# Two transformer blocks in one kernel: how the position bias gets its diagonals, and five places where TensorE waited

## The reference

```python
bias = rel_bias[t5_bucket(t[:, None] - s[None, :])]   # 16 heads, 256 distances
s = q @ k * HEAD_DIM ** -0.5 + bias
u = causal_depthwise_conv(a * sigmoid(gate), conv_w, conv_b)
u = silu(layer_norm(u, ln_g, ln_b))
c_q, c_kv = rmsnorm(c_q, ...), rmsnorm(c_kv, ...)     # block 2, latent stage
```

## Time and profile before

| | |
|---|---|
| median of 3 runs | 2812.84 us |
| profiled execution | 2812.7 us, span 2810.9 us |
| TensorE (PE) busy | 2788.9 us, 99% |
| VectorE (DVE), ScalarE (ACT), GpSimd (POOL) busy | 1949.3, 1377.6, 165.2 us |
| granted TensorE clock, mean | 0.999 |
| DMA, of 16 engines' span | hardware queue 59.5%, GpSimd's queue 0.2% |
| HBM read, written | 505.9 MB, 2.1 MB |

### The profile page before, as it was taken

One profiled execution on the slowest core, in us unless ns is written; L12 is line 12 of the kernel. 1 busy time (PEld: TensorE's weight loads), 2 busy tenths in 40 slices (PEclk: granted clock), 3 DMA queues, 4 the chain that ended last, 5 costly groups with the idle time before them and its releaser, 6 DMA issues.

```text
span 2810.9 us, 45292 instructions
## 1 busy us (share of the span) xinstructions
PE 2788.9 (99%) x15285; PEld 2388.5 (85%) x15285; DVE 1949.3 (69%) x2984; ACT 1377.6 (49%) x1865; POOL 165.2 (6%) x81
## 2 busy tenths in 40 slices
PE   8999999999999999999999999999999999999998
PEld 7888988888888888888888888888888888888887
DVE  6988787866885787778866777777655555555555
ACT  5336755544554455655544555554454434443444
POOL 6770010000000000000000000000000000000000
PEclk9999999999999999999999999999999999999999
DMA  9865365666665665655555565655566556555654
GB/s 246 211 160 130 95 175 184 186 209 189 187 191 193 185 192 189 185 146 152 160 184 177 174 183 172 180 172 187 190 202 190 189 191 195 188 189 194 190 190 154
DMA packets 506528, 509.64 MB, mean 181 GB/s; under 512 B 89662, under 2 KB 405934, under 8 KB 505902
## 3 DMA queue, kind: packets, MB, share of 16 engines
q1 hardware_dynamic: 505774, 506.01, 59.5%
q0 software_dynamic: 560, 2.12, 0.2%
q10 hardware_dynamic: 80, 0.01, 0.0%
HBM read 505.90 MB, written 2.12 MB: 181 GB/s over the span
## 4 chain that ended last, share of the span: by engine, by line
PE 99%; DVE 0%; ACT 0%; DMA 0%; issue 0%; ACTq 0%; SPq 0%; DVEq 0%
PE banks L1928 34%; PE banks L1931 17%; PE banks L1958 12%; PE banks L1959 12%; PE banks L1960 12%; PE banks L1943 3%; PE banks L1904 2%; PE banks L1945 1%; PE banks L1912 1%; PE banks L2194 1%; PE banks L1913 1%; PE banks L1914 1%; PE banks L2008 0%; PE banks L2325 0%; PE banks L2375 0%; PE banks L2129 0%
## 5 line engine op out<-in xcount | busy, mean ns | idle before, releaser
L602 ACT ACTIVATE w_two<-w_raw 128x1024 fp32r<-128x1024 f32 x944 | 995.1, 1059 | 1146.1 <-PE banks L1960 555.6
L1078 DVE TENSOR_TENSOR w_two<-w_raw,w_two 128x1024 fp32r<-128x1024 f32 (+1 forms) x881 | 1075.3, 1229 | 656.3 <-ACT w_two L602 650.5
L1928 PE MATMUL banks<-hp,w_two 128*128 128x512 f32 x3200 | 1014.1, 398 | 1.0 <-issue 1.0
L1931 PEld LDWEIGHTS banks<-hp,w_two 128*128 128x128 f32 x3200 | 601.4, 188 | 140.2
L1931 PE MATMUL banks<-hp,w_two 128*128 128x256 f32 x3200 | 632.0, 278 | 0.0
L1928 PEld LDWEIGHTS banks<-hp,w_two 128*128 128x128 f32 x3200 | 489.7, 189 | 9.3 <-issue 5.7
L1958 PE MATMUL banks<-w_two,yp 128*128 128x512 f32 x1056 | 412.1, 390 | 0.0
L1960 PE MATMUL banks<-w_two,yp 128*128 128x512 f32 x1056 | 411.2, 389 | 0.0
L1959 PE MATMUL banks<-w_two,yp 128*128 128x512 f32 x1056 | 411.1, 389 | 0.0
L1094 DVE TENSOR_REDUCE arena<-banks 128x256 f32<-128x512 f32 x304 | 195.1, 684 | 55.4 <-PE banks L1931 50.0
L1960 PEld LDWEIGHTS banks<-w_two,yp 128*128 128x128 f32 x1056 | 198.3, 188 | 41.3
(11 more groups left out here) (310 smaller groups left out, 2418.8 us busy)
## 6 DMA issues: line engine op xcount, KB each, us to landing
w_raw<-in_w_in SPq DMA_DIRECT2D x480, 256.0 KB, 3.1
w_raw<-in_w_up SPq DMA_DIRECT2D x352, 256.0 KB, 2.9
w_raw<-in_w_down SPq DMA_DIRECT2D x176, 256.0 KB, 3.0
w_raw<-in_w_ffn_gate SPq DMA_DIRECT2D x176, 256.0 KB, 2.8
w_raw<-in_w_ffn_up SPq DMA_DIRECT2D x176, 256.0 KB, 2.9
w_raw<-in_w_ffn_down SPq DMA_DIRECT2D x176, 256.0 KB, 3.2
w_raw<-in_w_out SPq DMA_DIRECT2D x128, 256.0 KB, 3.6
w_raw<-in_w_mla_proj SPq DMA_DIRECT2D x64, 256.0 KB, 3.0
```

What stands on the lines that cost most here:

```text
L602: nc.scalar.activation(w_hi[:, s, 0:n], w_raw[:, s, 0:n], ACT.Copy).then_inc(hi_ready, 1)
L1078: v.tensor_tensor(w_lo[:, s, 0:n], w_raw[:, s, 0:n], w_hi[:, s, 0:n].bitcast(f32), ALU.subtract)\
L1928: mm(banks[:, b, :], w_hi[:, s, at:at + P], rhs[:, k0 + k, :], start=k0 + k == kt_first, stop=False)
L1931: ins = mm(banks[:, b, 0:T], w_lo[:, s, at:at + P], rhs[:, k0 + k, 0:T], start=False, stop=k0 + k == kt_last)
```

## The change

The bias row is scaled at once and stored 128 times, one copy per partition (3.1 MB instead of 24 KB), ahead of unit kv 2; ahead of kv 20 GpSimd reads it with a step of 3 x 128 - 1 values, straight into `biasT`, in the right order. The flip products, their evictions and the matrix are gone, and VectorE waits for the read ahead of the first scores. Besides: (1) products on a tile of ones at the start and in the gaps of it, the fourth eviction of x0 and the first of x1 moved behind the statistics of x1, ScalarE's root ahead of an eviction; (2) the sums of the convolution's squares come one unit later; (3) the first unit of w_out_conv no longer waits for its bank; (4) GpSimd adds up the squares of the latent stage completely, so that `latent_sums` has 4 products instead of 12 and one that clears; (5) `queries(0)` comes ahead of the copy of the latent row.

```diff
-for _name, _cols in (("ident", P), ("flip", P), ("ones", P), ("cos", T), ("sin", T),
+for _name, _cols in (("ident", P), ("ones", P), ("cos", T), ("sin", T),
...
-        bias_d = nc.dram_tensor("bias_by_distance", (NQ, 3 * P), f32, kind="Internal").ap()
+        bias_d = nc.dram_tensor("bias_by_distance", (NQ, P, 3 * P), f32, kind="Internal").ap()
...
         @block.scalar
+            tiny_root(ROOT[0], x_var, x_root)
             later_half(1)
-            tiny_root(ROOT[0], x_var, x_root)
             later_half(2)
...
         @block.gpsimd
-                    if ph == "conv" and j == 7:
+                    if ph == "kv" and j == 2:
                         pool.wait_ge(sem("bias_row"), 1)
-                        pool.dma_start(bias_d, bias_row[0:NQ, :]).then_inc(sem("bias_stored"), 16)
-                    if ph == "conv" and j == 10:
+                        pool.dma_start(bias_d, bias_row[0:NQ, :].unsqueeze(1).to_broadcast([NQ, P, 3 * P])).then_inc(sem("bias_stored"), 16)
+                    if ph == "kv" and j == 20:
                         pool.wait_ge(sem("bias_stored"), 16)
-                        pool.dma_start(bias_win, bass.AP(bias_d.tensor, 0, [[1, P], [3 * P, NQ], [1, T]])).then_inc(loaded["bias"], 16)
+                        pool.wait_ge(sem("vec_copied"), 1)
+                        pool.dma_start(biasT, bass.AP(bias_d.tensor, P - 1, [[3 * P - 1, P], [3 * P * P, NQ], [1, T]])).then_inc(loaded["bias"], 16)
...
+            pool.wait_ge(sem("latent_summed"), QT // 2 - 1)
+            nc.gpsimd.tensor_tensor(latsq[:, 0, :], latsq[:, 0, :], latsq[:, 1, :], ALU.add).then_inc(sem("latent_summed"), 1)
+            pool.wait_ge(sem("latent_squares"), (QT + KVT) // 2)
+            nc.gpsimd.tensor_tensor(latsq[:, QT:QT + 2, :], latsq[:, QT:QT + 2, :], latsq[:, QT + 2:QT + 4, :], ALU.add)\
+                .then_inc(sem("latent_summed"), 1)
+            pool.wait_ge(sem("latent_summed"), QT // 2 + 1)
+            nc.gpsimd.tensor_tensor(latsq[:, QT, :], latsq[:, QT, :], latsq[:, QT + 1, :], ALU.add).then_inc(sem("latent_summed"), 1)
...
         @block.vector
+            v.memset(spare(0, T), 1.0).then_inc(sem("warm_tile"), 1)
             v.memset(zeros, 0.0).then_inc(sem("zeroed"), 1)
...
-            for g in range(4):
+            for g in range(3):
                 turned(0, g)
             dve.wait_ge(loaded["x1"], 16)
...
             v.tensor_scalar(x_var, x_sums, 1.0 / D, EPS, ALU.mult, ALU.add).then_inc(sem("variance"), 1)
-            turned(1, 0)
+            turned(0, 3)
             tiny_refine(ROOT[0], x_var, x_root, x_r).then_inc(sem("x_root"), 1)
...
             rooted(0, 0)
             rooted(0, 1)
+            turned(1, 0)
             lows("conv", 0, 0, 1)
...
-            v.tensor_copy(bias_row[0:NQ, 0:T], banks[0:NQ, 7, 0:T]).then_inc(sem("bias_row"), 1)
+            v.tensor_scalar(bias_row[0:NQ, 0:T], banks[0:NQ, 7, 0:T], HD ** 0.5, None, ALU.mult).then_inc(sem("bias_row"), 1)
...
-                if t >= 4:
-                    flipped(2 * t - 8)
-                    flipped(2 * t - 7)
...
             lo("q", 0, 11)
+            dve.wait_ge(loaded["bias"], 16)
             scores(0)
...
+            queries(0)
             dve.wait_ge(sem("latent_row"), 1)
             link(v.tensor_copy(r_kv, banks[:, 5, 0:T]))
...
-            queries(0)
             loop("mla", mla)
...
         @block.tensor
+            def warm(n, bank):
+
+                for _ in range(n):
+                    mm(banks[:, bank, 0:T], spare(0, T)[:, 0:P], spare(0, T), start=True, stop=True)
+
+            pe.wait_ge(sem("warm_tile"), 1)
+            warm(3, 1)
             pe.wait_ge(loaded["ident"], 16)
             pe.wait_ge(loaded["g0"], 16)
             turn(banks[:, 0, 0:KT], vec_rows[0:KT, 0, :], KT).then_inc(sem("gain_turned"), 1)
+            warm(2, 1)
             for b in range(QB):
...
+            pe.wait_ge(sem("x_transposed"), 1)
+            warm(3, 4)
             x_scaled(0, 6)
...
                 if t == 4:
-                    pe.wait_ge(loaded["bias"], 16)
                     pe.wait_ge(sem("vec_copied"), 1)
-                for k in range(2 * t - 8, 2 * t - 6) if t >= 4 else ():
-                    if k >= 2:
-                        pe.wait_ge(sem("bias_ready"), k - 1)
-                    mm(banks[:, 4 + k % 2, :], c_("flip"), bias_win[:, 2 * k:2 * k + 2, :], start=True, stop=True).then_inc(sem("bias_flipped"), 1)
...
                     if (g, u) == (0, 2):
                         pe.wait_ge(sem("conv_done"), 1)
                         sums(banks[:, 7, 0:T], conv_y, CT).then_inc(sem("conv_sum"), 1)
+                    if (g, u) == (1, 0):
+                        pe.wait_ge(sem("conv_squares"), 1)
+                        sums(banks[:, 7, T:], conv_sq, CT).then_inc(sem("conv_sum"), 1)
...
-                    pe.wait_ge(sem("conv_squares"), 1)
-                    sums(banks[:, 7, T:], conv_sq, CT).then_inc(sem("conv_sum"), 1)
...
-                if k1 == 0:
+                if k1 == 0 and n:
                     free("w_out_conv", 0, n)
...
-                mm(banks[:, 4, 0:4], ident, zeros, start=True, stop=False, skip_group_check=True)
-                for t in (0, 1, *range(QT, QT + KVT)):
-                    if t < QT:
-                        pe.wait_ge(sem("latent_summed"), QT // 2 - 1)
-                    else:
-                        pe.wait_ge(sem("latent_squares"), t // 2 + 1)
-                    at = 0 if t < QT else 2
+                for at, t, count in ((0, 0, QT // 2), (2, QT, QT // 2 + 2)):
+                    pe.wait_ge(sem("latent_summed"), count)
                     for b in range(QB):
                         ins = mm(banks[:, 4, at + b:at + b + 1], latsq[:, t, b * P:(b + 1) * P], ones[:, 0:1],
-                                 start=False, stop=t == QT + KVT - 1, skip_group_check=True)
+                                 start=at + b == 0, stop=True, skip_group_check=True)
```

More of the change, by code:

```diff
@@ L168, in constants @@
     put("ident", np.eye(P))
-    put("flip", np.eye(P)[::-1])
     half = ROPE // 2
@@ L381, in rows @@
             return ap[kt0 * P:(kt0 + n) * P].rearrange("(k p) n -> p k n", p=P)[:, :, cols]
-        bias_win = yp_f[:, 0:NQ * T].rearrange("p (h n) -> p h n", n=T)
         w1k, w1v = (yp_f[:, (NQ + 8 * kv) * T:(NQ + 8 * kv + 8) * T].rearrange("p (l n) -> p l n", n=HD) for kv in range(2))
@@ L1270, in taps @@
                     link(ins)
[L1272 to L1277, removed]
             def blocks(kv):
@@ L1624, in _, with queries @@
             link(rope(kpe, kraw, swap))
+            def queries(i):
+                used("mla", i, 2)
+                take(qn[:, 0, :], 0)
+                take(qn[:, 1, :], 1)
+                take(qraw, 2)
+            queries(0)
             dve.wait_ge(sem("latent_row"), 1)
@@ L1637, in maxima @@
                 v.tensor_scalar(m, m, scale, None, ALU.mult).then_inc(sem(name), 1)
[L1639 to L1644, removed]
             def mla(i, last):
@@ L2098, in _ @@
                     pe.wait_ge(loaded["cmp"], 16 * 12)
-                    pe.wait_ge(sem("bias_ready"), 8)
                     for kv in range(2):
```

## The result

2825.47 us (median of 6 runs, 2823.51 to 2826.48) against 2812.98 before (6 runs, 2811.35 to 2814.35): ratio 1.0044, 95% interval 1.0033 to 1.0054. The change makes the kernel 12.5 us slower; 11.2 us faster was predicted, and the range ended at 2821.

The account below looks back on a forecast made before the run. TensorE was taken to hold 99% of the chain of waits. The terms 6.3 + 1.0 + 0.4 + 0 + 4.3 - 0.8 = 11.2 us came off 2812.7, giving 2801.5 us, range 2799 to 2821.

Parts of the forecast that it names:

- flip products: Conv stage: eight products go, 4 x 1.72 = 6.9 us off TensorE, less a loss of 0.6; net gain 6.3 us.
- the 0.6 charged for unit 27: Conv unit 27, the tightest: weights 3.8 us earlier against TensorE 4.4 us earlier, a loss of 0.6 us.
- The store: New bias store ahead of kv 2, with its read at kv 20: 0.8 us lost, range 0 to 21.
- the 73 against 44 ns: w_out loads, time per 1 KB packet into 64 against 128 partitions; three such halvings put the store at 39 us.
- Rival (b): Store at 39 us, or two rows to a packet; units 38 to 42 wait, 21 us lost, 2822; chance 0.17.
- one packet for each of its packets: Rival at the store: weights take turns with slow packets, 27 us store, 9 us lost, 2810; chance 0.27.
- Start: Warm-up products and moved evictions bring the first unit from 18.50 to 17.5 us: gain 1.0, bounds 0.3 and 1.2.
- Squares: Squares of the convolution: the 1.3 us wait goes, but 1.0 returns at q 12; gain 0.4, bounds 0 and 1.4.
- w_out_conv: First unit's 1.6 us wait for its bank goes but moves to unit 1; gain 0, bounds 0 and 1.6.
- Latent stage: Eight short products stay of 26, no clock fall, queries(0) earlier: gain 4.3 us, bounds 2 and 4.5.

Follow-up runs that it names:

- reads by ScalarE: Changed kernel with 32 copies of the bias row out of partitions 0 to 15, four reads in a row at kv 20 issued by ScalarE: 2802.09 us.
- rows apart: Changed kernel, 128 copies out of partitions 0 to 15, with 16 values left free behind each row in DRAM: 2825.06 us, ratio 1.0047.
- five waits alone: Kernel before the change with only the five edits of the waits, bias and flip products the old way: 2808.59 us, ratio 0.9982.
- the half store: Changed kernel with 64 copies out of partitions 0 to 15 and two reads, at kv 17 and kv 20: 2811.59 us, ratio 0.9995.

## Why the prediction was wrong

**Bound, flip products.** TensorE's path sets the time; that held. The products brought 6.88 us, 4 x 1.72 in full, by unit 36; the 0.6 charged for unit 27 did not come. In ten of the other kernels without the flip products their absence brought 6.9 as well, in one (reads by ScalarE) 6.3: there TensorE did wait for a lo at unit 27, 0.3 us. The estimate was on the edge of what happens.

**The store: the step that failed.** "I take 0.8 us, nearest the only large GpSimd DMA there is": it cost 23.7. The old read went to all partitions; the store comes out of partitions 0 to 15, and the run out of 128 partitions (1.2 us lost) shows that this is the difference. Scaling up the 73 against 44 ns by three halvings gave 39 us against 34.5 measured; that bound was the better neighbour of the two. Rival (b) had the place (units 38 to 42; it was unit 38), the price (21 us; TensorE waited 20.8 in all) and the turning point (a store over 30 us), at a chance of 0.17. Its picture of the weights was not right: it let two to four units land beside the store, and one did not. From 114 to 142 us 0.3 MB of weights moved, less than one unit, and all that while unit 38 was on its way. Two things were missed. A packet of the store held three rows, not one or two (672 of 4608 B in place of 2048 of 1.5 KB), so that even "one packet for each of its packets" gives the weights 0.7 MB. And that rule was far too kind at first: in the 4 us from 116 the weights got 6 packets against 89. It held later: from 128 to 142 us they got 299 against 300.

**What the range left out.** All cases ended with the wait. The idle stretch also took the clock down: 5.5 us of unit 38 at 1.2 GHz, 2.5 us. With 1.6 more in w_out_conv and a start without its gain of 1.0 (both below) this is what lies beyond 2821.

**Start.** -1.0 predicted. +0.14 in the profiled execution of the changed kernel, -0.5 to -1.0 in ten other kernels with these products, -0.3 in one more. It goes with the clock, whose first record at full rate is at 10.2 us in the changed kernel, at 4.1 to 6.3 in those eleven and at 10.5 before. (In the one at -0.3, rows apart, the clock rose first of all, at 4.1, but x landed later: its second half was transposed from 9.53 us, with five waits alone from 8.96.) The window from 6 to 8 us in the changed kernel, then in the one with five waits alone:

```profile
6.00:8.00 2.00, 1.77 (x8) 1.42 (x8) 0.26 (x1) 1.44 (x1) 0.00 (x0) 1.00 0.99 413
```

```profile
6.00:8.00 2.00, 1.55 (x14) 1.55 (x15) 0.85 (x2) 1.57 (x1) 0.00 (x0) 1.00 1.01 419
```

The column of the granted clock prints 1.00 in both, for it has no record this early; the durations tell it: 8 transposes in 1.77 us, 221 ns each, against 14 in 1.55, 111 ns each. The changed kernel's clock was still low, and the products on ones had no effect in that execution. Why, with the same products from 1.20 us on, stays open.

**Squares.** -0.4 predicted, -0.3 seen: the wait goes (-1.4 by unit 64) and comes back at q 12 (+1.1; TensorE's wait there 0.8, predicted 1.0).

**w_out_conv.** 0 predicted. The wait moved to unit 1 as said: 1.9 us in place of 1.6. The idle of the weight loads there, after:

```profile
281.87 0.19 PEld L1912 LDWEIGHTS banks<-yp,w_two 128*128 128x128 f32 x1 [2.15 <-DVE x L1436]
```

1.4 us behind it the clock was 0.50 for 3.4 us. The same fall shows in seven of the thirteen profiles with this edit, and these lose 1.6 us from q 12 to w_out; it shows in none of the other six, and these lose 0.1, though all thirteen have the wait of 1.9. So the fall costs 1.5. It was not foreseen, and what brings it in the one and not in the other is not shown.

**Latent stage.** -4.3 predicted, -4.4 seen in every kernel: eight products in 0.79 us, and the granted clock was 1.00 in the row 1213 to 1217 above, where it was 0.57 before.

```profile
1213.81 0.79 PE banks L2294 x8
```

## What to carry to other kernels

Before moving bytes, ask which partitions they leave from: 3.1 MB out of partitions 0 to 15 held all DMA engines for 31 us (112 to 143) at 100 GB/s, and the stream that feeds TensorE stood still. A store like it should be spread over 128 partitions, cut into pieces shorter than what the stream has in hand (here some 10 us), or made smaller (a step of 3 x 128 - 4 and four reads need a quarter of the copies). When the trace has no row for a new transfer, weigh its bounds by what it has in common with each neighbour: here the partitions, not the queue.

## What was not expected of the hardware

- A slow packet costs every queue: at 94 to 100% share of the engines the store moved 100 GB/s, and the weights under 2 GB/s for 12 us (10 packets from 114 to 126 us), then some 21, one packet of 1 KB for each of 4608 B. Why the first 12 us were worse stays open; the half store had 18 to 24 GB/s beside it from 116 us on. SyncE, which mostly issues a load in 0.4 to 0.5 us, took 4.1 to 6.1 us for each between 113.6 and 141 us.
- With four DMAs issued by GpSimd, one add of VectorE over two SBUF operands took 7.9 to 11.5 us, where no such add took over 3.3 us in the other profiles (90 to 270 us).
- An idle TensorE pays twice: in six kernels waits of 5.0 to 7.7 us were followed by 6.8 to 13.7 us of 1.2 GHz, which took 1.7 to 5.5 us more.
